# A two-layer decoder trunk on one core: the order of the first norm, the first weight units and the first SiLUs

## What is computed

```python
h = x
for i in range(DEPTH):                      # DEPTH = 2
    h = h + 0.5 * swiglu(rmsnorm(h, ffn1_norm[i]), ffn1_w_gate[i], ffn1_w_up[i], ffn1_w_down[i])
    ...                                     # convolution and state-space mixer, W_out
    h = h + 0.5 * swiglu(rmsnorm(h, ffn2_norm[i]), ffn2_w_gate[i], ffn2_w_up[i], ffn2_w_down[i])
    ...                                     # per-layer embedding with a gate
return rmsnorm(h, final_norm)
```

## Time and profile before

| what | us |
|---|---|
| median of 3 runs | 1000.47 |
| lowest and highest | 999.67, 1000.62 |
| span of the profiled execution | 998.1 |
| PE busy in the span | 984.3 (99%) |
| DVE busy | 854.5 (86%) |
| ACT busy | 515.9 (52%) |
| POOL busy | 370.8 (37%) |

### The profile page before, as it was taken

How to read it: one execution, slowest core, us unless ns; L and a number is a source line. 1 busy time by engine, 2 the same in 40 slices (tenths; PEclk the granted TensorE clock), 3 DMA queues, 4 the chain that set the end, 5 groups by cost and what they waited for, 6 DMA issues and landing times.

```text
span 998.1 us, 16112 instructions
## 1 busy us (share of the span) xinstructions
PE 984.3 (99%) x5553; PEld 832.7 (83%) x5553; DVE 854.5 (86%) x1400; ACT 515.9 (52%) x728; POOL 370.8 (37%) x577
## 2 busy tenths in 40 slices
PE   9999999999999999999999999999999999999996
PEld 7788878899978888888877888888998788888885
DVE  6898999889879888996789978997998888787865
ACT  5444344585754444444555444445856454444453
POOL 6888999910137888980008600001002000000000
PEclk9999999999999999999999999999999999999999
DMA  9766556533546846464635565645344664655541
GB/s 291 218 210 209 169 171 207 169 128 128 183 158 201 262 151 227 155 223 169 211 127 177 195 217 168 210 168 169 128 169 139 199 210 165 214 179 199 200 159 43
DMA packets 143600, 181.63 MB, mean 182 GB/s; under 512 B 18432, under 2 KB 125632, under 8 KB 143552
## 3 DMA queue, kind: packets, MB, share of 16 engines
q1 hardware_dynamic: 142312, 179.65, 54.2%
q10 hardware_dynamic: 1240, 1.36, 0.4%
HBM read 179.93 MB, written 1.05 MB: 181 GB/s over the span
## 4 chain that ended last, share of the span: by engine, by line
PE 90%; DVE 6%; issue 2%; ACT 1%; DMA 0%; POOL 0%; POOLq 0%; DVEq 0%
PE ps L1539 29%; PE ps L1541 28%; PE ps L1540 28%; DVE hTf L930 2%; DVE wL L829 2%; PE ps L1554 2%; PE ps L1826 1%; PE ps L1792 1%; ACT wH L447 0%; PE ps L1856 0%; PE ps L1850 0%; PE ps L1836 0%; DVE uL L856 0%; DMA ctmp<-in_ffn_norm_dram 0%; DVE xres L870 0%
## 5 line engine op out<-in xcount | busy, mean ns | idle before, releaser
L829 DVE TENSOR_TENSOR wL<-raw,wH 128x1024 fp32r<-128x1024 f32 x334 | 421.6, 1308 | 23.9 <-ACT wH L447 22.8
L447 ACT ACTIVATE wH<-raw 128x1024 fp32r<-128x1024 f32 x334 | 334.1, 1050 | 81.9 <-PE ps L1541 80.4
L1539 PE MATMUL ps<-wH,uH 128*128 128x512 f32 x832 | 326.4, 392 | 1.7 <-DVE wL L829 1.2
L1541 PE MATMUL ps<-wH,uL 128*128 128x512 f32 x832 | 324.0, 389 | 0.0
L1540 PE MATMUL ps<-wL,uH 128*128 128x512 f32 x832 | 323.9, 389 | 0.0
L930 DVE STREAM_TRANSPOSE hTf<-bufB 32x128 f32<-32x128 f32 x640 | 193.8, 303 | 9.5
L1539 PEld LDWEIGHTS ps<-wH,uH 128*128 128x128 f32 x832 | 156.2, 188 | 36.7 <-DVE uL L856 3.0
L1541 PEld LDWEIGHTS ps<-wH,uL 128*128 128x128 f32 x832 | 156.2, 188 | 32.9
L1540 PEld LDWEIGHTS ps<-wL,uH 128*128 128x128 f32 x832 | 156.3, 188 | 31.4
L1539 PE MATMUL ps<-wH,hTH 128*128 128x512 f32 x352 | 138.2, 393 | 0.8 <-DVE wL L829 0.8
L1541 PE MATMUL ps<-wH,hTL 128*128 128x512 f32 x352 | 137.1, 390 | 0.0
(11 more groups left out here) (198 smaller groups left out, 1065.9 us busy)
## 6 DMA issues: line engine op xcount, KB each, us to landing
raw<-in_ffn_w_down_dram SPq DMA_DIRECT2D x88, 512.0 KB, 4.0
raw<-in_ffn_w_gate_dram SPq DMA_DIRECT2D x86, 512.0 KB, 4.0
raw<-in_ffn_w_up_dram SPq DMA_DIRECT2D x86, 512.0 KB, 5.0
raw<-in_w_in_dram SPq DMA_DIRECT2D x32, 512.0 KB, 4.4
raw<-in_w_out_dram SPq DMA_DIRECT2D x16, 512.0 KB, 3.8
raw<-in_ple_w_gate_dram SPq DMA_DIRECT2D x16, 512.0 KB, 4.1
raw<-in_glu_w_dram SPq DMA_DIRECT2D x4, 512.0 KB, 3.7
raw<-in_ple_w_proj_dram SPq DMA_DIRECT2D x4, 512.0 KB, 3.8
```

Source lines behind the costliest of these rows:

```text
L447: nc.scalar.activation(wH[:, slot, w], raw[:, slot, w], ACT.Copy).then_inc(wh_done, 1)
L829: nc.vector.tensor_tensor(wL[:, slot, w], raw[:, slot, w], wH[:, slot, w].bitcast(F32), ALU.subtract).then_inc((wl_half, wl_done)[a], 1)
L1539: mul(o, sH, vH, start=start, stop=False)
L1541: return mul(o, sL, vH, start=False, stop=stop)
```

## The change

On ACT, the first quarter of unit 0 is copied before quarter 0 of u, and the squares of tile 0 are taken before quarters 2 and 3 of u (they stood behind both halves of unit 1). On DVE, quarter 1 of u (gained(0, 0, 1)) goes behind all four quarters of unit 0, and rest(0, 0, 0) behind the first of them. Unit 3 is split in halves around the two SiLUs: ACT splits it between the SiLU of tile 0 and that of tile 1, DVE takes its first half between the two `hidden` multiplications. Unit 4 is split by ACT before `hidden_H`, and by DVE with its first half before `hidden_L` and its second behind it. PE's, POOL's and SP's programs are unchanged.

```diff
@@ ffn(l, f), scalar @@
                 if l + f == 0:
                     split_at(0, 2)
                 act.wait_ge(rs_done, rs_at(l, 2 * f))
-                if l + f == 0:
-                    silus(0, 0, 0, 1)
-                    split_at(0, 3)
-                else:
-                    silus(l, f, 0, base + 1, lambda: split_at(l, base + 3))
+                silus(l, f, 0, base + 1, lambda: split_at(l, base + 3))
...
-                def step(i):
-                    hidden_H(l, f, i - 1)
+                def step(i, split_first=False):
+                    if not split_first:
+                        hidden_H(l, f, i - 1)
                     for part in range(3):
                         if part == 2:
                             silus(l, f, i, i * 3 + base)
                         u = base + 1 + part
                         split(l, i * 3 + u, u % SLOTS, i + (u // SLOTS + 1))
+                        if part == 0 and split_first:
+                            hidden_H(l, f, i - 1)
                         if part == 0 and f == 0 and isinstance(i, int):
                             c_turned(l, 0)
...
-                step(1)
+                step(1, split_first=l + f == 0)
@@ first_norm, scalar @@
                 vectors(act, 0, slice(4, 7))
-                norm_H(0, 0, 0)
                 act.wait_ge(wt_used, 1)
                 for k in range(4):
                     if k < 3:
                         act.wait_ge((quarter_ld, first_ld, ld[0])[k], 32)
                     w = slice(512 * k, 512 * k + 512)
                     nc.scalar.activation(wH[:, 0, w], raw[:, 0, w], ACT.Copy).then_inc(wh_done, 1)
+                    if k == 0:
+                        norm_H(0, 0, 0)
                 norm_H(0, 0, 1)
                 vectors(act, 0, slice(7, 13))
+                squares(0, 0, 0)
                 norm_H(0, 0, 2)
                 norm_H(0, 0, 3)
                 split_at(0, 1)
-                squares(0, 0, 0)
                 squares(0, 0, 1)
@@ ffn(l, f), vector @@
                 if l + f == 0:
                     split_at(0, 2)
-                    hidden(0, 0, 0)
-                    split_at(0, 3)
+                    hidden(0, 0, 0, lambda: half_split(0, 3, 0, 0))
+                    half_split(0, 3, 0, 1)
...
                 def step(i, turned=True, params=False, split_first=False):
+                    if split_first:
+                        half_split(l, i * 3 + base + 1, (base + 1) % SLOTS, 0)
                     hidden_L(l, f, i - 1)
...
-                        if part < 2 or not split_first:
+                        if part == 0 and split_first:
+                            half_split(l, i * 3 + u, u % SLOTS, 1)
+                        elif part < 2 or not split_first:
                             split(l, i * 3 + u, u % SLOTS)
@@ first_norm, vector @@
                 gained(0, 0, 0)
-                gained(0, 0, 1)
-                rest(0, 0, 0)
                 for k in range(4):
                     w = slice(512 * k, 512 * k + 512)
                     dve.wait_ge(wh_done, k + 1)
                     nc.vector.tensor_tensor(wL[:, 0, w], raw[:, 0, w], wH[:, 0, w].bitcast(F32),
                                             ALU.subtract).then_inc((wl_quarter, wl_half, wl_quarter, wl_done)[k], 1)
+                    if k == 0:
+                        rest(0, 0, 0)
+                gained(0, 0, 1)
                 rest(0, 0, 1)
```

## The result

The changed kernel takes 1003.92 us (median of 5 runs, 1003.19 to 1004.50), the kernel before 1000.33 on the same chip: ratio 1.0038, interval 1.0027 to 1.0048. It is slower by 0.38%, about 3.6 us; the predicted time was 1002.2, 1.9 over before, inside the bound I had called indistinguishable, with 0.41 for slower. The measured time lies in the stated range of 1000.1 to 1004.3, but 0.9 above the range of my own case (1001.2 to 1003.0). The profiled execution's span is 1001.4, 3.3 us more than before.

A forecast was written before the change was run, and what follows sets the result against it. PE was taken to bound the kernel. Start 0, tile 1 +2.65, unit 4 -0.96 and the wait at 128.06 0 gave +1.7 on 1000.47: 1002.2 us, range 1000.1 to 1004.3.

The forecast's parts named there:

- my own case: The prediction's main course for the whole kernel: 1002.2 us, range 1001.2 to 1003.0, chance 0.59.
- The mechanism: Unit 0, tile 1: late gained(0, 0, 1) holds ACT's copy, six issues, squares and norm_H(0, 0, 2); PE +2.65 us.
- Tile 1, +2.65: PE starts tile 1 of unit 0 at 15.60 instead of 12.95, 2.65 us later.
- hidden, by 0.7 at least: POOL's pv_full, needing all thirteen small loads, ends at about 17.0 to 17.8, before PE wants it at 18.5.
- rival 4: Small loads come 1.5 us later, so PE waits at 18.5 for turn_vectors: about +0.8 us, 1003.0; chance 0.07.
- four signs of being wrong: Wrong if issues start before norm_H(0, 0, 1), matmuls 0.46 apart, turn_vectors waits for POOL, or 128.06's wait changes over 0.6.
- The wait near 128: PE's wait for DVE at 128.06: DVE and POOL move about the same, cost 0, bounds -0.6 and +0.6 us.
- Unit 4, -0.96: PE's wait at unit 4 for DVE's split disappears, taking back 0.96 us.
- whichever list DVE and ACT had: At unit 4, PE's lateness of 2.65 us would cover the 0.96 wait with either the old or new order.
- The start, 0 (at most 0.1): First gate-and-up matmul stays at about 8.64, since the fillers occupy PE: 0 won, upper bound 0.1 us.
- rival 1: Granted clock falls in PE's 3.1 us wait before tile 1, costing 1.7 us more: 1003.9; chance 0.16.
- rival 2: ACT's issues don't wait behind norm_H(0, 0, 1); PE starts tile 1 at 14.07, total +0.15 us, 1000.6; chance 0.10.

The follow-up runs named there:

- first_norm alone: The kernel before with only the first_norm hunks of the change, units 3 and 4 as before: 1003.43 us, ratio 1.0039.
- with the squares back: The changed kernel with squares(0, 0, 0) again behind unit 1's halves on ACT, directly ahead of squares(0, 0, 1): 1003.27 us, ratio 1.0035.
- the issues one place later: The kernel before with ACT's six small-vector issues behind norm_H(0, 0, 2) instead of ahead of it: 1005.77 us, ratio 1.0057.
- POOL's chain sooner: The kernel before with POOL's clearing of the taps moved ahead of the first rs: 999.58 us, ratio 0.9997.

## Why the prediction came out as it did

**The mechanism was right.** The late gained(0, 0, 1), the waiting copy, the six issues behind it, the squares behind those: each stands in the rows in the order and nearly at the times given (issues at 10.70 predicted, 11.00 measured; squares 13.15 and 13.57; tile 1 15.60 and 16.01). Of the two experiments that touch one link of this chain, one wins back 2.9 of the 3.6 us and the other all of it, and the one that builds the link into the kernel before makes it 5.7 slower.

**Tile 1, +2.65 predicted, +3.06 measured.** The third quarter's load came at 8.40 instead of 8.11 in this execution, the six issues took 2.52 instead of 2.41, and the chain passed both on. With first_norm alone, where that quarter came at 7.99, tile 1 started at 15.51, within 0.1 of the forecast.

**The step that failed: "hidden, by 0.7 at least".** I let the small loads land as long after their issue as before, 3.9 us at most; they took 6.0 (13.08 to 19.12, where POOL ends its wait). Three other kernels that issue them late show the same: 5.75 to 5.86 with first_norm alone, with the squares back and with the issues one place later. In the kernel before, the DMA engines were busy 0.67 of the time from 10.5 to 13.1, while the small loads landed. In the changed kernel they go out at the same time as units 2 and 3, p and the couplings, with the engines full from about 13 on. That this traffic is what slowed them was not tested by itself. The wait was rival 4, at 0.07 and 0.8 us; it cost 0.63 between 16.01 and 19.55. A row before turn_vectors that waits for POOL was one of my four signs of being wrong.

**The wait near 128, costed at 0, measured +0.5.** PE's lateness against before is 2.79 at unit 4 and 3.31 behind this wait; its idle row grew by 0.67, past the 0.6 that I had named as a sign of being wrong. The omission of six POOL operations removes this wait, so it needs them. It is 1.23 to 1.46 by starts in six of the seven kernels that have the part on units 3 and 4 and compute the full tables (0.96 in the seventh, with the squares back), against 0.79 in the kernel before and 0.81 in it with POOL's chain sooner.

**Unit 4, -0.96.** Right in size (0.99 alone). But the prediction took a gain at unit 4 as a gain at the end. Alone it was given back at 127 and 200. It also took the gain for PE's lateness, whichever list DVE and ACT had; first_norm alone kept 0.90 of the wait.

**The start, 0 (at most 0.1), measured -0.46.** The fillers' last matmuls ran at the full clock sooner (2.00 for the twelve instead of 2.43). I had read their end near 8.6 as fixed, but the same twelve took 1.50 to 2.43 in other executions. Over all kernels of these experiments the old order's first gate-and-up matmul starts at 8.32 to 8.74, most often after a wait for DVE's first quarter, and the new order's at 7.86 to 8.21. So the new order is worth about 0.4 at the start, and nothing at the end, since tile 1's wait took it up.

**The sum.** +3.06 at tile 1, +0.63 at turn_vectors, +0.11 in restarting behind it, -1.01 at unit 4, +0.52 near 128: 3.31, the distance of the spans. I had +1.7; the forecast was too small by the second wait, by the wait near 128 and by 0.4 of the first. My case's range was also added up unevenly: its upper end has the 0.6 that I allowed near 128, its lower end doesn't.

**The rivals.** The clock did not fall in the changed kernel's profiled execution, though PE rested there for 3.44 us; it did fall after about as long a rest with first_norm alone (3.42; 0.50 from 16.9 to 20.0), after one of 3.98 with the issues one place later, and after a shorter one with the squares back (2.67). So the rival is real, and the length of the rest alone doesn't decide it; in the squares-back kernel its price was mostly covered by the wait for pv_full that followed. The profiled execution is also the fastest of the changed kernel's five runs. In three of them, the median among these, the mean granted clock was 0.994 or 0.995, and they took 1003.92 to 1004.50; the other two had 0.997 and 0.998 and took 1003.19 and 1003.73. In the 75 runs of the kernel before, beside the experiments, it was never under 0.997. So rival 1, to which I gave 0.16, probably came true in most runs and holds some 0.5 us of the 3.6; no trace of those runs was kept, so where the clock fell is not shown. The other two may have had a fall as well, since profiled executions with one had means of 0.996 and 0.997. The stated range held because it had taken in rivals 1 and 4, and both came true in part.

The issues did wait, so rival 2 is out. The rule of the Trainium skill (Advanced Engine Details and Errata, "Sequencer Loop") that a waiting instruction stands in the engine's queue while the sequencer goes on does not hold for what these traces show on ACT where the wait isn't yet satisfied: DMA issues start within 0.01 us of the last compute instruction ahead of them that had to wait, at 4.89, 8.10, 11.00 and 11.47 in three kernels. Where nothing is left to wait for, the traces agree with it: in the kernel before the issue at 8.10 ran ahead of two copies that stood before it in ACT's list and started at 8.63 and 9.15.

What stays open is why POOL's chain lost the 1.92 us it was given by starting sooner. Its small operations of 16 columns take 0.20 beside DVE's transposes and about 1.05 beside its subtractions in the same trace, which would tie POOL's place to DVE's; this was read, not tested.

## What to carry to other kernels

Before an operation is made later, look at who waits for it on another engine and what is queued behind that waiting instruction, DMA issues included: a wait that was already satisfied costs nothing, and once it isn't, everything behind it pays. Small loads issued later can also land later by more than the delay, as here, where the gap in the traffic that they had used was over. And a gain at one point of a bound engine is no gain until it has passed the next place where two engines share something; read the next two or three waits and ask of each what it is tied to.

## What the runs showed of the hardware

- On ACT, six small DMA issues took 2.4 to 2.6 us (0.25 to 0.49 each), and an operation whose input was ready stood behind them: ACT was idle for 1.94 us in the changed kernel and 2.01 with the issues one place later, marked "issue".
- A DVE operation with two inputs beside a POOL operation is slowed, and POOL's too: rest of 128x512 took 1.57 beside POOL and 0.69 without, POOL's 128x512 operation 1.90 beside DVE's split and 1.04 when it began just before the split, under the transposes' end. DVE's block transposes were not slowed (16 took 5.04 to 5.06 in all kernels). The Trainium skill (GPSIMD Engine Reference, the table of section 1) says that the two engines share their SBUF interfaces, with contention when a DVE instruction has two SBUF inputs; the traces agree.
- The granted clock fell to 0.50 after rests of PE of 2.67 us in one kernel, 3.42 in another and 3.98 in a third, and stayed at 1.00 through one of 3.44 in a fourth.
